# Strassen products for 14 of 22 column chunks of two FFN projections, with their weight sums made by DMA

## The chip, the cores and the metric

The kernel runs on one core of a Trainium2 chip. The metric is device time in microseconds for one launch; the time before is the median of three runs.

## The reference

Two transformer blocks run one after the other on one sequence of 512 tokens with 1024 features. The change lies in the gated feed-forward part, which occurs twice (layer 0 and layer 1):

```python
def conv_gated_ffn(x, w_up, w_gate, conv_w, conv_b, w_down):
    u = x @ w_up
    g = causal_dwconv(x @ w_gate, conv_w, conv_b)
    return (jax.nn.silu(g) * u) @ w_down
```

Here `x` is 512 x 1024, `w_up` and `w_gate` are 1024 x 2816, `w_down` is 2816 x 1024, and the convolution has three taps along the tokens. Everything is float32.

## The kernel before

**Layout.** Activations lie transposed: features on the 128 partitions, tokens along the row. `X` has 8 chunks of 128 features (index `k`), and 2816 columns are 22 chunks of 128 (index `f`). Every float32 operand is split into a rounded high part and a rest (`XH`, `XL`; `wh`, `wl`), and one product of a 128 x 128 weight block is three matmuls: high x high, high x low, low x high. `block` issues these three.

**The weight stream.** All weight blocks are laid out in HBM in the order in which TensorE (PE) uses them (`weight_order`, `ffn_order`), eight blocks (a unit, 512 KB) at a time. SyncE (SP) loads unit u into one of three buffers `wraw`, once unit u-3 has been split. ScalarE (ACT) rounds it to `wh` (`round_to`), VectorE (DVE) subtracts to get `wl` and raises the semaphore `w_lo`; there are four slots of `wh`/`wl`. Both engines do so at fixed places of their own programs: `feed_group` over blocks makes the unit three ahead (`AHEAD`) wherever the listed blocks cross the start of a unit. So a unit is split late if the engine is held up by the work written ahead of it.

**The FFN.** For each f PE makes 8 blocks of `up` and 8 blocks of `gate` into two of six PSUM banks. Then comes what I call the gating of f: ACT applies the middle tap to the gate bank, DVE adds the other two taps (two operations), ACT applies Silu, DVE multiplies by the up bank, ACT rounds the result to `HH`, DVE subtracts to get `HL`. The FFN is preceded by a projection `pg` (64 blocks), and by a layer norm, whose sums over the chunks are added by GpSimd (POOL) into `acc_s` as the chunks of `X` appear, then summed over the partitions by PE (`means`).

**Order.** All five programs are written out by hand, each engine runs its own strictly in order, and they meet at semaphores alone.

Of the kernel before, what the change touches and what calls it, by code (L numbers as in the profile page):

```python
# [15 lines left out]
KD = 8  # L16
# [5 lines left out]
ALPHA = 4.0 ** 0.25  # L22
TAPS = 31
# [100 lines left out]
class Stream:  # L124


    def __init__(self):
# [33 lines left out]
    def depth(self, m):  # L161
        return FT if m[:4] == "down" else 2 if m[:2] in ("pp", "uq") else 1 if m[:3] == "ukv" else KD
# [84 lines left out]
class Semaphores:  # L247
    def __init__(self, new):
# [13 lines left out]
        self.first_in, self.blank = n("first_in"), n("blank")  # L262
# [20 lines left out]
            n("f_u"), n("f_conv"), n("f_silu"), n("f_h"), n("f_hi"), n("f_lo"))  # L283

# [51 lines left out]
def place(nc, ctx, m):  # L336
# [47 lines left out]
    m.PP, m.HH, m.HL, m.pts = [], [], [], []  # L384
    for layer in range(2):
        with ExitStack() as ph:
            with ExitStack() as same:
                m.PP.append(sb(same, f"PP{layer}", [128, KD, S]))
            m.HH.append(sb(ph, f"HH{layer}", [128, FT, S], FR))
            with ExitStack() as same:  # L390
                m.pts.append(sb(same, f"pts{layer}", [128, 2, S]))
            m.HL.append(sb(ph, f"HL{layer}", [128, FT, S], FR))
# [26 lines left out]
    with ExitStack() as ph:  # L419
# [15 lines left out]
        m.pick, m.pick2 = sb(ph, "pick", [128, 128], FR), sb(ph, "pick2", [128, 128], FR)  # L435
    m.sba = [[sba[:, c] for _, c, _ in GR], [x[:, 0:c.stop - c.start] for x, (_, c, _) in zip((m.sqr[0], m.acc_q, m.acc_s), GR)]]
# [42 lines left out]

def unit(m, w, u):  # L480
# [7 lines left out]
def sync_program(sp, m, s, w, a):  # L488
    def raw(u):
# [4 lines left out]
        sp.e.dma_start(m.wraw[u % RAW][:, :], a["wstream"][u]).then_inc(s.raw[u % RAW], 16)  # L494
# [8 lines left out]
    def pt(layer):  # L503
        for k in range(2):
            sp.e.dma_start(m.pts[layer][:, k, :], a["pt"][layer][:, k * S:(k + 1) * S]).then_inc(s.pt_in[2 * layer + k], 16)

    x(0, 1, s.x_in[0])
    first(0, s.first_in)
# [7 lines left out]
    sp.e.dma_start(m.prm[:, :], a["params"]).then_inc(s.p_in, 16)  # L516
    sp.e.dma_start(m.cst[:, :], a["consts"]).then_inc(s.c_in, 16)
    for u in range(3, w.units):
# [12 lines left out]
        if u == w.at["in0", 0, 0] // NU + AHEAD + RAW:  # L531
            sp.wait_ge(s.nrm_u, normed(4, 7))
            for r in range(64, 128, 16):
                sp.e.dma_start(m.wgu[r:r + 16, :, :], a["wgu"].rearrange("l p n -> p l n")).then_inc(s.g_in, 16)
# [8 lines left out]
    for c in range(KD):  # L543
        sp.wait_ge(s.xsum, 48 + c + 1)
        sp.e.dma_start(a["o"][:, c * S:(c + 1) * S], m.X[:, c, :]).then_inc(s.out, 16)
    sp.wait_ge(s.out, 16 * KD)


def tensor_program(pe, m, s, w):
# [142 lines left out]
    def ffn(layer, i):  # L692
# [18 lines left out]
        for f in range(FT):  # L711
            bu, bg = bank[(2 + 2 * f) % 6], bank[(3 + 2 * f) % 6]
            if f < 3:
                pe.wait_ge(s.pg_u, 8 * layer + 4 + 2 * f)
# [4 lines left out]
            if f >= 3:  # L719
# [52 lines left out]
    pe.wait_ge(s.blank, 1)  # L772
# [539 lines left out]
def scalar_program(act, m, s, w, nc):  # L1312
# [92 lines left out]
    def embed_in(layer):  # L1405
        for k in range(2):
            act.wait_ge(s.pt_in[2 * layer + k], 16)
            fn(m.HH[layer][:, FT - 2 + k, :], m.pts[layer][:, k, :], ACT.Copy).then_inc(s.pt_hi, 1)

    def ffn(layer, i):  # L1410
# [9 lines left out]
        for f in range(FT):  # L1420
            n = FT * layer + f
            u, v = tmp[2 * f % 4], tmp[(2 * f + 1) % 4]
            bg = bank[(3 + 2 * f) % 6]
            feed_group(f"up{layer}", range(KD), [f])
            feed_group(f"gate{layer}", range(KD), [f])
            act.wait_ge(s.stream, w.done(f"gate{layer}", KD - 1, f))
# [1679 lines left out]
```

## Time and profile before

| | |
|---|---|
| median of three runs | 1748.67 us (1748.43 to 1748.83) |
| span of the profiled execution | 1747.5 us |
| what the median has over that span | 1.2 us |
| PE busy | 1736.9 us (99%) |
| DVE busy | 1063.6 us (61%) |
| ACT busy | 847.1 us (48%) |
| POOL busy | 18.4 us (1%) |
| granted TensorE clock | 1.000 |
| DMA, mean | 89 GB/s |

The span is from the first to the last instruction of one execution. Durations below come from that execution, and a difference of spans is set on the median. The busy time of PE is the union of overlapping matmuls, so the pace of PE is read from the distance between the starts of two matmuls, not from the duration of one.

### The profile page before, as it was taken

To read this page: it belongs to the slowest core of one execution; us is meant where nothing else is said; L and a number is where in the kernel's file an instruction comes from. 1 tells how busy PE (TensorE), PEld (TensorE's weight loads), DVE (VectorE), ACT (ScalarE), POOL (GpSimd) and SP (SyncE) were. 2 spreads that over 40 slices of the span, in tenths; PEclk is the share of its full clock that TensorE was granted. 3 is DMA by queue.
4 is the path that set the end of the run, shared out by engine and by line. 5 is a ranking of instruction groups with operands and counts; after the bars stand their busy time and mean duration, and the time that the engine had idled before them with its cause. 6 is when DMAs were issued, how large, how long until landed. Compare 5 with 4: busy or idle time off the path is not lost.

```text
span 1747.5 us, 22538 instructions
## 1 busy us (share of the span) xinstructions
PE 1736.9 (99%) x9213; PEld 1409.7 (81%) x9213; DVE 1063.6 (61%) x1666; ACT 847.1 (48%) x1330; POOL 18.4 (1%) x21
## 2 busy tenths in 40 slices
PE   9999999999999999999999999999999999999999
PEld 7887988888888897777778888888898866778766
DVE  6788864444433465877784444443378866656674
ACT  7789643333332355666463333342255455534542
POOL 0000100000000000000200000000000000000000
PEclk9999999999999999999999999999999999999999
DMA  5331232222222321111132232323213221132111
GB/s 216 110 121 45 89 109 97 97 97 97 97 97 96 97 85 61 62 58 51 61 112 96 96 98 95 101 90 109 97 61 107 96 70 63 61 97 97 61 60 49
DMA packets 44678, 155.43 MB, mean 89 GB/s; under 512 B 5280, under 2 KB 5536, under 8 KB 44576
## 3 DMA queue, kind: packets, MB, share of 16 engines
q1 hardware_dynamic: 44576, 153.99, 26.6%
q8 instruction: 73, 1.20, 0.3%
q14 instruction: 29, 0.24, 0.0%
HBM read 149.78 MB, written 2.10 MB: 87 GB/s over the span
## 4 chain that ended last, share of the span: by engine, by line
PE 90%; ACT 4%; DVE 4%; issue 1%; DMA 1%; SPq 0%; DVEq 0%; ACTq 0%
PE bank L553 89%; ACT tmp L1316 2%; DVE tmp L1990 1%; DVE wl L1999 1%; DMA wraw<-in_wstream 1%; ACT taps L1316 1%; ACT wh L1316 1%; PE bank L1261 0%; DVE XL L1999 0%; DVE sbl L1999 0%; ACT HL L1316 0%; DVE HL L1999 0%; ACT Y L1316 0%; DVE X L1987 0%; DVE acc_q L1987 0%
## 5 line engine op out<-in xcount | busy, mean ns | idle before, releaser
L553 PE MATMUL bank<-XH,wh 128*128 128x512 f32 (+1 forms) x1504 | 583.4, 388 | 3.7 <-ACT wh L1316 1.1
L553 PE MATMUL bank<-XL,wh 128*128 128x512 f32 (+1 forms) x1504 | 573.5, 382 | 0.0
L553 PE MATMUL bank<-XH,wl 128*128 128x512 f32 (+1 forms) x1504 | 573.5, 382 | 0.0
L1999 DVE TENSOR_TENSOR wl<-wraw,wh 128x1024 fp32r<-128x1024 f32 (+1 forms) x264 | 319.6, 1220 | 237.8 <-ACT wh L1316 237.2
L1316 ACT ACTIVATE wh<-wraw 128x1024 fp32r<-128x1024 f32 (+1 forms) x264 | 276.2, 1052 | 250.4 <-PE bank L553 242.7
L553 PEld LDWEIGHTS bank<-XH,wh 128*128 128x128 f32 x1504 | 282.8, 188 | 68.7 <-issue 9.3
L553 PEld LDWEIGHTS bank<-XH,wl 128*128 128x128 f32 x1504 | 282.8, 188 | 55.2
L553 PEld LDWEIGHTS bank<-XL,wh 128*128 128x128 f32 x1504 | 283.0, 188 | 52.3 <-issue 0.7
L1987 DVE SCALAR_TENSOR_TENSOR tmp<-bank,prm,tmp 128x511 f32<-128x511 f32 x88 | 65.9, 749 | 172.1 <-ACT tmp L1316 170.6
L553 PE MATMUL bank<-HH,wh 128*128 128x512 f32 (+1 forms) x420 | 155.7, 371 | 0.0
L553 PE MATMUL bank<-HH,wl 128*128 128x512 f32 (+1 forms) x420 | 154.1, 367 | 0.0
L553 PE MATMUL bank<-HL,wh 128*128 128x512 f32 (+1 forms) x420 | 154.0, 367 | 0.0
L1316 ACT ACTIVATE tmp<-bank,prm 128x512 f32<-128x512 f32 (+1 forms) x64 | 46.2, 723 | 193.0 <-PE bank L553 192.9
L1316 ACT ACTIVATE tmp<-tmp 128x512 f32<-128x512 f32 (+2 forms) x131 | 72.4, 595 | 86.3 <-DVE tmp L1987 85.8
L553 PEld LDWEIGHTS bank<-HH,wh 128*128 128x128 f32 x420 | 79.2, 189 | 13.8 <-issue 0.6
L553 PEld LDWEIGHTS bank<-HL,wh 128*128 128x128 f32 x420 | 79.2, 189 | 13.5 <-issue 0.5
L553 PEld LDWEIGHTS bank<-HH,wl 128*128 128x128 f32 x420 | 79.2, 189 | 13.0
L1316 ACT ACTIVATE tmp<-bank 128x512 f32<-128x512 f32 (+4 forms) x129 | 70.8, 567 | 17.8 <-PE bank L553 15.3
L1990 DVE TENSOR_TENSOR X<-X,bank 128x512 f32<-128x512 f32 (+1 forms) x58 | 38.5, 665 | 40.0 <-PE bank L553 40.0
L553 PE MATMUL bank<-XH,HL 128*128 128x256 f32 x256 | 57.4, 287 | 0.3 <-DVE XL L1999 0.2
L553 PE MATMUL bank<-wh,XH 128*128 128x512 f32 x128 | 50.7, 396 | 0.1
L553 PE MATMUL bank<-wh,XL 128*128 128x512 f32 x128 | 49.9, 390 | 0.0
(350 smaller groups left out, 2181.9 us busy)
## 6 DMA issues: line engine op xcount, KB each, us to landing
wraw<-in_wstream SPq DMA_DIRECT2D x276, 512.0 KB, 3.5
out<-X SPq DMA_DIRECT2D x8, 256.0 KB, 2.3
X<-in_xt SPq DMA_DIRECT2D x3, 512.0 KB, 8.9
pts<-in_pt SPq DMA_DIRECT2D x4, 256.0 KB, 3.7
eb<-lab SPq DMA_DIRECT2D x16, 64.0 KB, 2.0
cst<-in_consts SPq DMA_DIRECT2D x1, 810.5 KB, 10.1
X<-in_xt SPq DMA_DIRECT2D x2, 256.0 KB, 4.2
wraw<-in_wstream SPq DMA_DIRECT2D x2, 256.0 KB, 4.8
```

Source lines behind the costliest of these rows:

```text
L553: return pe.e.matmul(o, l, r, start=start, stop=stop, skip_group_check=True)
L1316: return act.e.activation(o, i, f, **kw)
L1987: return dve.e.scalar_tensor_tensor(out=o, in0=i0, scalar=sc, in1=i1, op0=op0, op1=op1)
L1990: return dve.e.tensor_tensor(o, i0, i1, op)
L1999: return dve.e.tensor_tensor(o, x, h.bitcast(F32), ALU.subtract)
```

## The change

For the first 14 chunks (seven pairs f, f+1) of both projections, the 2 x 2 product of halves is made with seven quarter products instead of eight. The halves are: features 0 to 511 and 512 to 1023, tokens 0 to 255 and 256 to 511, chunk f and chunk f+1. A quarter product is four blocks on 256 tokens. Three things are needed for it:

- **Sums of weights.** Four arrays T1 to T4 are formed in HBM (`tw`) by POOL's DMA queue. For each layer there are eleven transfers of one quarter of the weights of all 14 pairs of both matrices (14 x 128 x 512 floats, 3.67 MB): four copies, then four, two and one that accumulate, each stage waiting for the one before. They stand in POOL's program ahead of the sums of the layer norm. The stream then takes the blocks `tu` and `tg` from `tw`, and SP waits for all eleven ahead of the first of them.
- **Sums of activations.** DVE forms four sums of quarters of X (`SF`, `SG`), ACT and DVE split them into `XS`, in rows of `HH` and `HL` that the FFN does not use yet.
- **Combining.** Per pair and matrix, ACT copies two quarters out of PSUM, DVE does five additions of 256 tokens, and the results lie in SBUF (`sqr` for up, `acc_s` and `acc_q` for gate). The gating reads them there in place of the banks, and is done for both chunks of a pair in the next pair.

The blocks of a pair go from 32 on 512 tokens to 56 on 256 tokens, so the units of the stream go from 4 to 7 a pair.

```diff
 def ffn_order(layer):
     out = []
-    for f in range(FT):
+    for p in range(PAIRS):
+        f, (up, gate), (tu, tg) = 2 * p, (f"up{layer}", f"gate{layer}"), (f"tu{layer}", f"tg{layer}")
+        out += [(up, k, f) for k in range(KD)]
+        if p:
+            out += [(gate, k, f - 1) for k in range(4, KD)]
+        out += [(tu, k, p) for k in range(16)] + [(gate, k, f) for k in range(KD)]
+        out += [(up, k, f + 1) for k in range(4, KD)] + [(tg, k, p) for k in range(16)]
...
 def sync_program(sp, m, s, w, a):
...
-        sp.e.dma_start(m.wraw[u % RAW][:, :], a["wstream"][u]).then_inc(s.raw[u % RAW], 16)
+        for c0, c1, summed in w.pieces(u):
+            if summed:
+                mat, k, p = w.order[NU * u + c0 // 128]
+                layer = int(mat[2:])
+                sp.wait_ge(s.tw, 176 * (layer + 1))
+                src = a["tw"][k // 4, layer, p + PAIRS * (mat[1] == "g")]
...
 def tensor_program(pe, m, s, w):
...
+        def last_product(g, p):
+            pe.wait_ge(s.u_c, combined(layer, p, g, 3))
+            pe.wait_ge(s.xs_l, 4 * layer + 4)
+            product(("up", "gate")[g] + str(layer), 2 * p + 1, 4, bank[3 * g + 1][:, lo], sums_of(3), False, True)
+
+        for p in range(PAIRS):
+            first_products(0, p)
+            if p:
+                last_product(1, p - 1)
+            summed_products(0, p)
+            first_products(1, p)
+            last_product(0, p)
+            summed_products(1, p)
...
 def vector_program
...
+        for p in range(PAIRS):
+            f = 2 * p
+            feed_group(up, range(KD), [f])
+            if p:
+                gated(f - 2, sqr[0], m.gb[0])
+            first_combined(0, p)
+            if p:
+                feed_group(gate, range(4, KD), [f - 1])
+                last_combined(1, p - 1)
+                gated(f - 1, sqr[1], m.gb[1])
+            feed_group(tu, range(16), [p])
+            three_combined(0, p)
+            feed_group(gate, range(KD), [f])
+            first_combined(1, p)
+            feed_group(up, range(4, KD), [f + 1])
+            last_combined(0, p)
+            dve.wait_ge(s.u_c, combined(layer, p, 0, 5))
+            feed_group(tg, range(16), [p])
+            three_combined(1, p)
...
 def gpsimd_program
+    def weight_sums(layer):
+
+        t1, t3, t4, t2 = (a["tw"][t, layer].rearrange("n p c -> (n p) c") for t in range(4))
+        w11, w12, w21, w22 = (a[n][layer].rearrange("n p c -> (n p) c") for n in ("w11", "w12", "w21", "w22"))
+        pool.wait_ge(s.w_lo, (6, 60)[layer])
+        for t in (t1, t3, t2, t4):
+            pool.e.dma_start(t, w12).then_inc(s.tw, 16)
+        pool.wait_ge(s.tw, 176 * layer + 64)
+        for t, x in ((t1, w11), (t3, w22), (t2, w22), (t4, w22)):
+            pool.e.dma_start(t, x, accum_op=ALU.add, max_dma_last_dim=8192).then_inc(s.tw, 16)
+        pool.wait_ge(s.tw, 176 * layer + 128)
+        for t in (t2, t4):
+            pool.e.dma_start(t, w11, accum_op=ALU.add, max_dma_last_dim=8192).then_inc(s.tw, 16)
+        pool.wait_ge(s.tw, 176 * layer + 160)
+        pool.e.dma_start(t4, w21, accum_op=ALU.add, max_dma_last_dim=8192).then_inc(s.tw, 16)
```

The programs of DVE in the FFN of layer 0 show what now lies in a row. Before, in the stretch of two chunks (one pair), four splits of units (`wl`) and two gatings:

```order
L1999 TENSOR_TENSOR wl1<-wraw1,wh1 128x1024 [waits s_w_hi]
L1999 TENSOR_TENSOR wl2<-wraw2,wh2 128x1024 [waits s_w_hi]
L1987 SCALAR_TENSOR_TENSOR tmp0<-bank1,prm,tmp0 128x511 [waits s_f_u]
L1987 SCALAR_TENSOR_TENSOR tmp0<-bank1,prm,tmp0 128x510 [waits s_dve]
L1990 TENSOR_TENSOR tmp1<-tmp0,bank0 128x512 [waits s_f_silu]
L1999 TENSOR_TENSOR HL0<-tmp1,HH0 128x512 [waits s_f_hi]
```

After, the same engine from the last addition behind one pair's `tg` blocks to the point at which the next pair's `up` blocks of chunk f+1 may start (the first two rows of `three_combined(0, p)` stand last):

```order
L2140 TENSOR_TENSOR acc_s<-acc_s,bank5 128x256
L2149 TENSOR_TENSOR wl3<-wraw2,wh3 128x1024 [waits s_w_hi]
L2137 SCALAR_TENSOR_TENSOR tmp0<-acc_s,prm,tmp0 128x511 [waits s_f_u]
L2137 SCALAR_TENSOR_TENSOR tmp0<-acc_s,prm,tmp0 128x510 [waits s_dve]
L2140 TENSOR_TENSOR tmp1<-tmp0,sqr0 128x512 [waits s_f_silu]
L2149 TENSOR_TENSOR HL0<-tmp1,HH0 128x512 [waits s_f_hi]
L2140 TENSOR_TENSOR sqr0<-sqr0,bank0 128x256 [waits s_u_e]
L2140 TENSOR_TENSOR acc_q<-bank4,acc_q 128x256 [waits s_stream]
L2137 SCALAR_TENSOR_TENSOR tmp2<-acc_q,prm,tmp2 128x511 [waits s_f_u]
L2137 SCALAR_TENSOR_TENSOR tmp2<-acc_q,prm,tmp2 128x510 [waits s_dve]
L2140 TENSOR_TENSOR tmp3<-tmp2,sqr1 128x512 [waits s_f_silu]
L2149 TENSOR_TENSOR HL0<-tmp3,HH0 128x512 [waits s_f_hi]
L2149 TENSOR_TENSOR wl0<-wraw0,wh0 128x1024 [waits s_w_hi]
L2149 TENSOR_TENSOR wl1<-wraw1,wh1 128x1024 [waits s_w_hi]
L2140 TENSOR_TENSOR sqr0<-sqr1,bank1 128x256 [waits s_u_e]
L2140 TENSOR_TENSOR sqr1<-bank1,sqr0 128x256 [waits s_u_c]
```

Both gatings now stand in one row of DVE's program, with three splits and four additions, ahead of the two additions on which PE waits.

POOL's program, from its start, which had nothing ahead of the first `acc_s` row before:

```order
L3152 DMA tw<-in_w12 64x14336 [waits s_w_lo]
L3152 DMA tw<-in_w12 64x14336 x3
L3155 DMA tw<-in_w11 448x2048 [waits s_tw]
L3155 DMA tw<-in_w22 448x2048 x3
L3158 DMA tw<-in_w11 448x2048 [waits s_tw]
L3158 DMA tw<-in_w11 448x2048
L3160 DMA tw<-in_w21 448x2048 [waits s_tw]
L3136 ISA
L3136 TENSOR_TENSOR acc_s<-X 128x512 [waits s_nrm_u,s_xsum]
```

The layer norm's first sum now stands behind the wait for ten of the eleven transfers.

## Rows read from the trace of the kernel before

**Rows 1.** The page: the span, and busy time of each engine

```profile
span 1747.5 us, 22538 instructions
PE 1736.9 (99%) x9213; PEld 1409.7 (81%) x9213; DVE 1063.6 (61%) x1666; ACT 847.1 (48%) x1330; POOL 18.4 (1%) x21
```

**Rows 2.** The page's chain that ended last, by engine and by line

```profile
PE 90%; ACT 4%; DVE 4%; issue 1%; DMA 1%; SPq 0%; DVEq 0%; ACTq 0%
PE bank L553 89%; ACT tmp L1316 2%; DVE tmp L1990 1%; DVE wl L1999 1%; DMA wraw<-in_wstream 1%; ACT taps L1316 1%; ACT wh L1316 1%; PE bank L1261 0%; DVE XL L1999 0%; DVE sbl L1999 0%; ACT HL L1316 0%; DVE HL L1999 0%; ACT Y L1316 0%; DVE X L1987 0%; DVE acc_q L1987 0%
```

**Rows 3.** Timeline of PE in the FFN (start us, duration us): matmuls of 512

```profile
336.78 0.39 PE L553 MATMUL bank<-XH,wl 128*128 128x512 f32 x1
337.01 0.39 PE L553 MATMUL bank<-XH,wh 128*128 128x512 f32 x1
```

**Rows 4.** Timeline of PE near 163 us: matmuls of 256, 24 apart

```profile
162.80 0.28 PE L553 MATMUL bank<-XH,HL 128*128 128x256 f32 x1
...
165.68 0.28 PE L553 MATMUL bank<-XH,wl 128*128 128x256 f32 x1
```

**Rows 5.** Timeline of DVE in the FFN, one chunk and the next gating

```profile
338.02 1.54 DVE L1987 SCALAR_TENSOR_TENSOR tmp<-bank,prm,tmp 128x511 f32<-128x511 f32 x2 [3.88 <-ACT tmp L1316]
...
341.64 0.69 DVE L1999 TENSOR_TENSOR HL<-tmp,HH 128x512 fp32r<-128x512 f32 x1 [0.70 <-ACT HH L1316]
342.59 2.43 DVE L1999 TENSOR_TENSOR wl<-wraw,wh 128x1024 fp32r<-128x1024 f32 x2 [0.26 <-ACT wh L1316]
348.90 1.53 DVE L1987 SCALAR_TENSOR_TENSOR tmp<-bank,prm,tmp 128x511 f32<-128x511 f32 x2 [3.88 <-ACT tmp L1316]
351.13 0.69 DVE L1990 TENSOR_TENSOR tmp<-tmp,bank 128x512 f32<-128x512 f32 x1 [0.70 <-ACT tmp L1316]
352.52 0.69 DVE L1999 TENSOR_TENSOR HL<-tmp,HH 128x512 fp32r<-128x512 f32 x1 [0.70 <-ACT HH L1316]
```

**Rows 6.** Timeline of ACT, the first step of the same gatings

```profile
337.21 0.78 ACT L1316 ACTIVATE tmp<-bank,prm 128x512 f32<-128x512 f32 x1 [4.32 <-PE bank L553]
348.09 0.78 ACT L1316 ACTIVATE tmp<-bank,prm 128x512 f32<-128x512 f32 x1 [4.32 <-PE bank L553]
```

**Rows 7.** Groups by shape over the span, DVE and ACT (busy us, mean ns)

```profile
L1999 DVE TENSOR_TENSOR wl<-wraw,wh 128x1024 fp32r<-128x1024 f32 x262 | 318.2, 1224 | 237.3 <-ACT wh L1316 236.6
L1987 DVE SCALAR_TENSOR_TENSOR Y<-cin,prm,Y 128x512 f32<-128x512 f32 x16 | 12.0, 752 | 0.3
L1990 DVE TENSOR_TENSOR X<-X,bank 128x256 f32<-128x256 f32 x4 | 1.7, 418 | 8.3 <-PE bank L553 8.3
L1316 ACT ACTIVATE acc_s<-bank 128x256 f32<-128x256 f32 x8 | 3.0, 379 | 0.0
```

**Rows 8.** The page on DMA: the queue of the stream, issue to landing

```profile
q1 hardware_dynamic: 44576, 153.99, 26.6%
wraw<-in_wstream SPq DMA_DIRECT2D x276, 512.0 KB, 3.5
```

**Rows 9.** Windows: busy of each engine, clock, DMA share, GB/s

```profile
30.00:178.00 148.00, 146.33 (x1151) 117.80 (x1144) 119.86 (x174) 125.37 (x195) 0.00 (x0) 1.00 0.28 92
250.00:440.00 190.00, 190.00 (x840) 157.39 (x839) 94.07 (x109) 71.40 (x89) 0.00 (x0) 1.00 0.29 95
```

**Rows 10.** Timeline of POOL in the layer norm ahead of layer 0's FFN

```profile
178.36 1.30 POOL L2926 TENSOR_TENSOR acc_s<-X 128x512 f32<-128x512 f32 x1 [177.92 <-DVE X L1987]
181.42 1.68 POOL L2926 TENSOR_TENSOR acc_s<-acc_s,X 128x512 f32<-128x512 f32 x1 [1.76 <-DVE X L1987]
186.37 1.73 POOL L2926 TENSOR_TENSOR acc_s<-acc_s,X 128x256 f32<-128x256 f32 x2 [0.96 <-DVE X L1987]
```

**Rows 11.** Timeline of PE: the sum of `acc_s` over the partitions

```profile
190.97 0.59 PE L553 MATMUL bank<-acc_s,cst 128*128 128x256 f32 x2
```

**Rows 12.** Timeline of DVE: splits of units 6 and 7, and ahead of layer 0's FFN

```profile
29.18 2.35 DVE L1999 TENSOR_TENSOR wl<-wraw,wh 128x1024 fp32r<-128x1024 f32 x2
...
226.15 2.35 DVE L1999 TENSOR_TENSOR wl<-wraw,wh 128x1024 fp32r<-128x1024 f32 x2
...
234.00 2.35 DVE L1999 TENSOR_TENSOR wl<-wraw,wh 128x1024 fp32r<-128x1024 f32 x2
```

**Rows 13.** Timeline of ACT: it waits for PE to leave a slot

```profile
244.79 1.06 ACT L1316 ACTIVATE wh<-wraw 128x1024 fp32r<-128x1024 f32 x1 [4.38 <-PE bank L553]
```

More of the change, by code:

```diff
@@ L22 @@
 ALPHA = 4.0 ** 0.25
+PAIRS = 7
+XS0 = 14
 TAPS = 31
@@ L42, in ffn_order @@
     out = []
-    for f in range(FT):
+    for p in range(PAIRS):
[5 more added lines that the diff above has]
+        out += [(up, k, f + 1) for k in range(4, KD)] + [(tg, k, p) for k in range(16)]
+    f = 2 * PAIRS
+    out += [(f"up{layer}", k, f) for k in range(KD)] + [(f"gate{layer}", k, f - 1) for k in range(4, KD)]
+    out += [(f"gate{layer}", k, f) for k in range(KD)]
+    for f in range(2 * PAIRS + 1, FT):
         out += [(f"up{layer}", k, f) for k in range(KD)] + [(f"gate{layer}", k, f) for k in range(KD)]
@@ L170, in done, with pieces, landed @@
         return self.total[p] - (3 - i if self.incs[p] == 4 else 0)
+    def pieces(self, u):
+        sums = [(b := self.order[NU * u + 4 * h]) is not None and b[0][:2] in ("tu", "tg") for h in range(2)]
+        return [(0, NU * 128, False)] if not any(sums) else [(512 * h, 512 * h + 512, sums[h]) for h in range(2)]
+    def landed(self, u):
+        return 16 * sum(len(self.pieces(v)) for v in range(u % RAW, u + 1, RAW))
     def used(self, u):
@@ L221, in half_at, with sums_of_pair, combined @@
     return sum(TAIL[j] + SPLIT[j] for j in range(1, i) if PARTS[j] == 2 and j != 3)
+def sums_of_pair(p):
+    return [(p, 0, 1)] + [(p - 1, 1, 5)] * (p > 0) + [(p, 0, 2), (p, 0, 3), (p, 0, 4), (p, 1, 1), (p, 0, 5), (p, 1, 2), (p, 1, 3), (p, 1, 4)]
+SUMS = [x for p in range(PAIRS) for x in sums_of_pair(p)] + [(PAIRS - 1, 1, 5)]
+def combined(layer, p, mat, j):
+    return 10 * PAIRS * layer + SUMS.index((p, mat, j)) + 1
 def normed(i, f):
@@ L388, in place @@
                 m.PP.append(sb(same, f"PP{layer}", [128, KD, S]))
+                m.SF.append([x[:, i, :, :] for x in [sb(same, f"SF{layer}", [128, 3, 4, 256])] for i in range(3)])
             m.HH.append(sb(ph, f"HH{layer}", [128, FT, S], FR))
@@ L391, in place @@
                 m.pts.append(sb(same, f"pts{layer}", [128, 2, S]))
+                sb(same, f"between{layer}", [128, 6, S])
+                m.SF[layer].append(sb(same, f"SG{layer}", [128, 4, 256])[:, :, :])
             m.HL.append(sb(ph, f"HL{layer}", [128, FT, S], FR))
@@ L435, in place @@
         m.pick, m.pick2 = sb(ph, "pick", [128, 128], FR), sb(ph, "pick2", [128, 128], FR)
+    m.XS = [[(m.HH, m.HL)[j // 2][layer][:, XS0 + 4 * (j % 2):XS0 + 4 * (j % 2) + 4, :] for j in range(4)] for layer in range(2)]
+    m.gb = [m.acc_s, m.acc_q]
     m.sba = [[sba[:, c] for _, c, _ in GR], [x[:, 0:c.stop - c.start] for x, (_, c, _) in zip((m.sqr[0], m.acc_q, m.acc_s), GR)]]
@@ L710, in ffn, with product @@
                     block(f"pg{layer}", k, c, bank[c][:, :], XH[:, k, :], XL[:, k, :], k == 0, k == KD - 1)
[L711 to L714, printed above, removed]
-            else:
+        lo, hi = slice(0, 256), slice(256, 512)
+        def product(mat, c, k0, o, x, first, last):
+            for k in range(k0, k0 + 4):
+                xh, xl = x(k)
+                block(mat, k, c, o, xh, xl, first and k == k0, last and k == k0 + 3)
@@ L716, in ffn @@
+        for f in range(2 * PAIRS, FT):
+            bu, bg = bank[(2 + 2 * f) % 6], bank[gate_bank(f)]
+            if f == 2 * PAIRS:
+                pe.wait_ge(s.u_c, combined(layer, PAIRS - 1, 0, 5))
+            elif f == 2 * PAIRS + 1:
+                pe.wait_ge(s.u_e, 4 * PAIRS * (layer + 1))
+                pe.wait_ge(s.u_c, 10 * PAIRS * (layer + 1))
+            elif f >= 2 * PAIRS + 3:
                 pe.wait_ge(s.f_h, FT * layer + f - 2)
@@ L1419, in ffn, with gated @@
                 fn(tmp[c % 4][:, :], bank[c][:, :], ACT.Sigmoid).then_inc(s.pg_u, 1)
-        for f in range(FT):
+            if f0 == 0:
+                for j in range(4):
+                    act.wait_ge(s.xs_f, 4 * layer + j + 1)
+                    fn(m.XS[layer][j][:, :, 0:256], m.SF[layer][j], ACT.Copy).then_inc(s.xs_h, 1)
+        up, gate, tu, tg = f"up{layer}", f"gate{layer}", f"tu{layer}", f"tg{layer}"
+        def gated(f, g):
             n = FT * layer + f
             u, v = tmp[2 * f % 4], tmp[(2 * f + 1) % 4]
[L1423 to L1426, printed above, removed]
             act.wait_ge(s.pg_x, 8 * layer + 8)
@@ L3014, in lay_out @@
     for n, w in enumerate(order):
-        if w is not None:
+        if w is not None and w[0][:2] not in ("tu", "tg"):
             m, k, c = w
```

168 lines of the change are left out of this document (137 added, 31 removed).

## The prediction

> **What bounds the kernel now.** I read the page first: PE is busy for 1736.9 of 1747.5 us, while DVE has 61% and ACT 48% [rows 1]. The chain that ended last says the same, 90% of it is PE, 89% one line, the matmul helper [rows 2]. So time is gained only by giving PE less to do, and lost as soon as another engine makes PE wait. Next I read the pace of PE from the starts of its matmuls. In the FFN, DVE's first tap of one chunk starts at 338.02 and that of the next at 348.90, so a chunk takes 10.88 us for its 48 matmuls of 512 tokens, 0.2267 us each; two neighbouring starts, 336.78 and 337.01, agree [rows 3, 5]. Matmuls of 256 tokens run 24 in 2.88 us, 0.120 us each [rows 4]. In the FFN PE is busy without a gap, 190.00 of 190 us; DVE is busy for half of it [rows 9].
>
> **What PE saves.** Per pair and matrix there were 16 blocks x 3 x 0.2267 = 10.88 us, now 28 x 3 x 0.120 = 10.08 us. The 256-token matmul costs 53% of the 512 one, so of the eighth that Strassen saves not quite 7.4% is left. Both matrices: 21.76 down to 20.16 us a pair, 14 pairs in two layers, 22.4 us if nothing ever waits.
>
> **DVE's row in a pair.** From the order of the programs: PE may start the last product of `up` (4 blocks) only when DVE has done the first two additions of `three_combined(0, p)`, and these stand behind both gatings of the pair before. The row starts when PE ends the 16 blocks of `tg`. Let that be 0, and price each step:
> - ACT copies a quarter out of PSUM: 0.20 us until it starts (the matmul that starts at 336.78 gives its place up at 337.01, ACT starts at 337.21 [rows 3, 6]), 0.38 for the copy [rows 7], 0.05 to reach DVE: 0.63.
> - Three additions of 256, at 0.42 [rows 7], 1.3 with their own waits.
> - One split of a unit. It occupies DVE for 1.22, and the next can start after 1.15: 1.15. ACT's rounding is done under the additions, and so is its first tap.
> - The gating of the first chunk, from DVE's first tap at 348.90 to the end of its last step at 353.21: 4.31, of it two waits of 0.70 for ACT [rows 5]. The taps read SBUF now; a tap from SBUF takes 0.752, from a bank 0.77, so that gives nothing [rows 5, 7].
> - Two additions of 256: 0.8.
> - The gating of the second chunk. ACT's first tap needs the addition just made, so it counts from ACT's start, 348.09 to 353.21: 5.12, and 0.08 for the handover [rows 5, 6].
> - Two splits: in the rows the two end 2.70 us after the gating before them (342.33 to 345.02), since ACT rounds them only after its part of the gating [rows 5].
> - Two additions: 0.9. Then 0.1 to PE.
>
> The sum is 0.63 + 1.3 + 1.15 + 4.31 + 0.8 + 5.2 + 2.7 + 0.9 + 0.1 = 17.1 us. PE reaches the same point after 8 blocks of `up`, 4 of `gate`, 16 of `tu` and 8 of `gate`, 36 x 0.36 = 12.96 us. It waits 4.1 us. After that it has 4 + 16 blocks to the end of `tg`, 7.2 us, and the row starts again; DVE's work in that part (four splits, three additions, 6.2 us) is hidden under it. So a pair takes 24.3 us, a closed loop of DVE and PE, against 21.76 before. What had covered the gating before was that nothing on DVE was needed by PE before the banks came round, a whole chunk later (DVE waited 3.88 us per chunk [rows 5]).
>
> Per layer: the first pair has no gating ahead of it and runs at PE's pace, 52 x 0.36 = 18.7 us. Six pairs take 6 x 24.3 = 145.8. The last product of `gate` is 1.4. Together 165.9 against 7 x 21.76 = 152.3, **+13.6 us a layer, +27 in both**. The eight chunks left run as before.
>
> **Sums of activations.** Four additions and four subtractions of 1024 elements on DVE, 8 x 1.22 = 9.8 us, stand ahead of the split that starts at 234.00 [rows 7, 12]. That unit is then ready at 234.0 + 9.8 + 1.2 = 245.0. PE ends its units at ACT's waits, 244.79 less some 0.1, and needs it there [rows 13]: 0.3 us. I take 1 us for both layers; it would be 10 us a layer if that cover were gone.
>
> **Sums of weights.** They start when the sixth unit has been split. The two splits at 29.18 are the sixth and seventh, so at 30.4 us [rows 12]. POOL can begin the layer norm's sums when ten transfers have landed, 36.7 MB. It began them at 178.36, and PE used the sum at 190.97; POOL's last addition had ended at 188.10, so 2.9 us are spare [rows 10, 11]. No row shows a transfer from HBM to HBM, nor one that accumulates. Bounds:
> - From below: a byte costs what it costs the stream. 153.99 MB took 26.6% of 1747.5 us, 331 GB/s at full use [rows 1, 8]. 36.7 MB are 111 us, and the stream takes 0.28 of the engines meanwhile [rows 9], so 154 us: done at 184 us. POOL's row of 1.3, 1.7, 1.7 and 0.9 follows: 190. PE waits for nothing.
> - From above: an accumulating transfer fetches what lies there too, so its bytes count twice. 14.7 + 2 x 22.0 = 58.7 MB are 177 us. From 30.4 to 191 us, 0.72 x 161 = 116 of them get done; then PE stands, the stream stops, and 61 are left: 252 us, POOL's row to 258, PE late by 67 us.
>
> I take the upper one, rounded to 60, because the sum cannot be made without reading both. A delay here is not made up: PE is always busy. The eleventh transfer is done some 22 us after the tenth and the stream asks for it later: before, the unit three behind it was split at 228.5 [rows 12], 37 us after PE's place at 190.97, so it costs nothing more.
>
> The Trainium skill, page "DMA: Bandwidth & Descriptors", section "Latency and other measured facts", has copies between two HBM tensors at 207 to 214 GB/s at best. An estimate from it: 36.7 MB, each byte once, would be 172 us, 116 of them by 191, the rest to 247 us, a delay of 62 us even if accumulation cost nothing. No run so far shows that rate; it speaks for the upper bound, by another way.
>
> **Layer 1's sums** start at the sixtieth unit, in the third pair of layer 0's FFN. In a pair of 24.3 us the stream now moves 7 units (3.67 MB), 151 GB/s or 0.46 of 331, where it took 0.29 before [rows 9]; a unit lands 3.5 us after its issue [rows 8]. DVE splits the last units of a pair in a burst with some 4 us for a load, so a landing twice as long costs 1 to 2 us a pair: 5 us in all, between 0 and the crowding below. They end long before layer 1's layer norm, some 540 us later.
>
> **Sum.** 27 + 1 + 60 + 5 = 93 on the span of 1747.5, which with its 1.2 is the median: **about 1842 us**.
>
> **The rivals.**
> - *The transfers are in time, DVE's loop alone costs:* 1748.7 + 28 = 1777 us. It needs the lower bound of the rate. Chance 0.22.
> - *The transfers crowd the stream.* A copy is cut into 64 rows of 57 KB, an accumulating one into rows of 8 KB (the order shows 64x14336 and 448x2048), the stream's packets are 153.99 MB / 44576 = 3.5 KB [rows 8]. If an engine takes one piece of each in turn, the stream has 4/61 of the engines while the copies run (14.7 MB, 44 us): two units land where layer 1's copies meet a demand of 13. With 3 in hand that is 8 x 3.5 = 27 us; in layer 0, at 5.44 us a unit, some 16. Beside the accumulating ones the stream gets 1/3, 110 GB/s, or 1/5, 66 GB/s, against 151: on some 22 units 1.3 to 4.5 us each, 29 to 98 us. Together 1842 + 72 to 140, 1914 to 1982 us. For it: nothing but the sizes. Against it: if the engines share by bytes, the stream's half (165 GB/s) is enough. Chance 0.15. (The Trainium skill, same page, section "Queues, rings and completion order": an engine goes round its queues packet by packet. That is this rival's rule; no row here has two busy queues.)
> - *Faster.* PE never waits in a pair: 1748.7 - 22 = 1726 us. It needs the row of 17.1 us to shrink to 12.96, and all transfers in time; the change breaks even at a row of 14.6 us. Nothing in the rows is 2.5 us shorter than I took it, the seven long waits and operations are read straight from the same code. Chance 0.09.
> - *No change,* by a row of 14 to 15 us and transfers in time: 0.04.
>
> **How the numbers follow.** The forecast, a delay of 40 to 80 us beside DVE's loop, has 0.50: 1815 to 1865. A range for 8 in 10 takes in the first rival, half the way to the second's upper end: 1765 to 1935. A measurement of this kernel tells about 0.2% from no change (3.5 us): faster 0.09, the same 0.04, slower 0.87.
>
> **What would show it.** In the profile after: PE's idle time before the first matmul of `up`'s last product (`HL` as the moving operand, 256 tokens) in each pair, released by DVE's additions, some 4 us each, twelve times; gatings of one pair back to back on DVE; starts of `tg` rows 24.3 us apart. POOL's first `acc_s` row at 240 to 255 us instead of 178, and PE standing for about 60 us at the sum of `acc_s`. Landings of the stream longer than 3.5 us between 30 and 250 us. I am wrong if POOL's first row stays near 180 (then 1777), or if gaps show before matmuls whose releaser is a split of a unit or a DMA (then crowding, above 1900).

## The result, and the profile after

The changed kernel takes 1977.41 us (median of four runs, 1975.26 to 1978.57), against 1748.74 for the one before on the same chip. The ratio is 1.1306, 95% interval 1.129 to 1.1322: 13% slower, 229 us. I had said 1842, with 1935 as the upper end.

The page after, the lines that answer to [rows 1, 2, 8]:

```profile
span 1975.3 us, 25036 instructions
...
PE 1771.6 (90%) x10221; PEld 1490.1 (75%) x10221; DVE 1179.4 (60%) x1864; ACT 914.7 (46%) x1436; POOL 36.5 (2%) x43
...
PEclk9898999866789999999999998899999999999999
...
q1 hardware_dynamic: 60704, 176.02, 27.6%
q0 software_dynamic: 7136, 80.74, 16.9%
...
PE 69%; DMA 15%; DVE 9%; ACT 5%; issue 1%; SPq 0%; POOL 0%; ACTq 0%; DVEq 0%; POOLq 0%
```

PE is busy for 90% of the span instead of 99%, and 15% of the chain that ended last is now DMA, which had 1% in [rows 2]. A new queue, q0, stands beside the stream's q1: POOL's transfers. The row of the granted clock, which read 9 throughout before, falls to 6 in the ninth and tenth of the 40 slices, and that is where PE stands most.

To see where the 229 us went, I set the same work side by side at two places that every kernel here has: POOL's first addition of each layer norm. POOL's timeline after (start, duration, the wait ahead in brackets):

```profile
31.72 2.19 POOL L3152 DMA_DIRECT2D tw<-in_w  x4 [31.27 <-DVE wl L2149]
80.81 4.03 POOL L3155 DMA_DIRECT2D tw<-in_w  x4 [46.91 <-DMA tw<-in_w]
172.41 1.97 POOL L3158 DMA_DIRECT2D tw<-in_w  x2 [87.56 <-DMA tw<-in_w]
214.67 0.97 POOL L3160 DMA_DIRECT2D tw<-in_w  x1 [40.29 <-DMA tw<-in_w]
225.91 1.29 POOL L3136 TENSOR_TENSOR acc_s<-X 128x512 f32<-128x512 f32 x1 [10.27 <-DVE X L2137]
...
364.36 2.04 POOL L3152 DMA_DIRECT2D tw<-in_w  x4 [108.44 <-DVE wl L2149]
413.63 4.01 POOL L3155 DMA_DIRECT2D tw<-in_w  x4 [47.23 <-DMA tw<-in_w]
...
1060.50 1.30 POOL L3136 TENSOR_TENSOR acc_s<-X 128x512 f32<-128x512 f32 x1 [519.85 <-DVE X L2140]
```

The first sum starts at 225.91 instead of 178.36 [rows 10]: 47.5 us are lost before layer 0's FFN. But look at what released it. It waited 10.27 us for DVE's `X`; ten transfers had landed at 214.67, eleven us earlier. So POOL's place in the order, my term of 60 us, did not bind. Between the two sums lie 834.6 us; before, 684.4. The rest of the kernel, with layer 1's FFN in it, lost another 30 us.

The same kernel's DMA window from 31 to 81 us, while the four copies run:

```profile
q0 software_dynamic: 320, 14.68, 81.2%
q1 hardware_dynamic: 606, 2.23, 14.9%
...
wraw<-in_wstream SPq DMA_DIRECT2D x6, 512.0 KB, 24.1
```

And the chain that ended last, its first DMA steps (start, duration):

```profile
32.56 25.39 DMA wraw<-in_wstream
60.32 22.84 DMA wraw<-in_wstream
85.53 17.98 DMA wraw<-in_wstream
...
365.59 47.57 DMA wraw<-tw
415.97 16.95 DMA wraw<-tw
435.28 29.15 DMA wraw<-in_wstream
```

Six units of the stream were loaded in 50 us with a median of 24.1 us from the issue of a load to its landing (the moment at which all of it has arrived), where [rows 8] have 3.5; the kernel before loaded ten in the same window. PE waits at a landing again and again. That is the crowding, my rival with 0.15. In layer 0's pairs one load from `tw`, half a unit (256 KB), took 47.57 us. PE's share there, by windows:

```profile
365.00:562.00 197.00, 80.39 (x504) 78.26 (x504) 53.31 (x77) 36.25 (x50) 8.37 (x10) 0.66 1.01 261
1123.00:1298.00 175.00, 149.09 (x1123) 146.92 (x1121) 116.54 (x165) 83.24 (x115) 0.00 (x0) 0.91 0.44 138
1189.70:1194.50 4.80, 4.77 (x22) 4.77 (x23) 3.33 (x5) 1.06 (x1) 0.00 (x0) 0.50 0.87 295
1194.50:1201.50 7.00, 7.00 (x60) 7.00 (x60) 3.54 (x5) 3.17 (x4) 0.00 (x0) 1.00 0.49 160
```

The columns are window, length, PE, PEld, DVE, ACT, POOL, granted clock, DMA share, GB/s. While layer 1's transfers run, PE works 80 of 197 us, at a mean clock of 0.66, and the DMA engines are full at 261 GB/s. The second window is some six pairs of layer 1, where no transfer of POOL's runs. There the pair as such can be seen, in PE's timeline:

```profile
1189.73 0.80 PE L606 MATMUL bank<-HL,wh 128*128 128x256 f32 x2 [4.35 <-DVE sqr L2140]
...
1216.70 0.80 PE L606 MATMUL bank<-HL,wh 128*128 128x256 f32 x2 [4.37 <-DVE sqr L2140]
```

The wait stands where I put it, released by whom I said, 4.35 us long where I had 4.1. But a pair takes 26.97 us, not 24.3. The last two windows show the missing part: in the 4.8 us behind the wait the granted clock is 0.50, the lower of its two levels (1.2 GHz), and PE gets 22 matmuls done; in the next 7 us it is 1.00, with 60 matmuls.

### The profile page after: what moved, and what is told of

Same layout as the page of the kernel before. It is cut to its first block, busy times and chain, and to the rows that moved or that the text cites. A ratio compares the mean times of both kernels' runs of the same rounds, so it can differ in the third digit from the quotient of the medians.

```text
span 1975.3 us, 25036 instructions
## 1 busy us (share of the span) xinstructions
PE 1771.6 (90%) x10221; PEld 1490.1 (75%) x10221; DVE 1179.4 (60%) x1864; ACT 914.7 (46%) x1436; POOL 36.5 (2%) x43
## 4 chain that ended last, share of the span: by engine, by line
PE 69%; DMA 15%; DVE 9%; ACT 5%; issue 1%; SPq 0%; POOL 0%; ACTq 0%; DVEq 0%; POOLq 0%
PE bank L606 68%; DMA wraw<-in_wstream 10%; DMA wraw<-tw 5%; DVE wl L2149 3%; ACT wh L1425 2%; ACT tmp L1425 2%; DVE tmp L2137 1%; DVE tmp L2140 1%; DVE sqr L2140 1%; DVE HL L2149 0%; PE bank L1370 0%; ACT HH L1425 0%; DVE acc_q L2140 0%; ACT taps L1425 0%; DVE X L2137 0%
## 5 line engine op out<-in xcount | busy, mean ns | idle before, releaser
L606 PE MATMUL bank<-XH,wh 128*128 128x512 f32 (+1 forms) x1392 | 507.7, 365 | 8.9 <-DVE wl L2149 6.4
L606 PE MATMUL bank<-XL,wh 128*128 128x512 f32 (+1 forms) x1392 | 497.3, 358 | 0.0
L606 PE MATMUL bank<-XH,wl 128*128 128x512 f32 (+1 forms) x1392 | 496.8, 357 | 0.0
L606 PE MATMUL bank<-HL,wh 128*128 128x256 f32 (+1 forms) x868 | 255.6, 345 | 145.3 <-DVE acc_q L2140 79.3
L606 PEld LDWEIGHTS bank<-HL,wh 128*128 128x128 f32 x868 | 163.6, 210 | 162.0 <-DVE acc_q L2140 80.0
L606 PE MATMUL bank<-HH,wh 128*128 128x256 f32 (+1 forms) x868 | 254.4, 344 | 6.6 <-DVE sqr L2140 3.3
L606 PE MATMUL bank<-HH,wl 128*128 128x512 f32 (+1 forms) x644 | 224.3, 348 | 0.0
L606 PEld LDWEIGHTS bank<-HH,wh 128*128 128x128 f32 x868 | 162.3, 209 | 21.2 <-DVE sqr L2140 3.5
L1425 ACT ACTIVATE tmp<-bank 128x512 f32<-128x512 f32 (+4 forms) x129 | 70.4, 566 | 15.4 <-PE bank L606 13.2
L606 PE MATMUL bank<-HL,wl 128*128 128x256 f32 x224 | 71.5, 319 | 0.0
L606 PEld LDWEIGHTS bank<-HL,wl 128*128 128x128 f32 x224 | 51.4, 229 | 0.0
```

Source lines behind the costliest of these rows:

```text
L606: return pe.e.matmul(o, l, r, start=start, stop=stop, skip_group_check=True)
L1425: return act.e.activation(o, i, f, **kw)
```

## The experiments

Where a number of a kernel is compared with its neighbour's, both are read at the same places: "front" is the start of the first `acc_s` sum in layer 0, "middle" the distance from it to that of layer 1, which holds layer 0's FFN. Before they are 178.36 and 684.4, after 225.91 and 834.6. "Kernel 1" is the kernel of experiment 1, and so on. Kernels 2, 3, 7, 9 and 10 were run once each, so their small differences carry little: the change and kernel 7 have the same program up to the 60th unit, and still their fronts are 8 us apart.

**1. Without the transfers.** `tu` and `tg` are read straight from quarters of the weights in HBM, not summed, so that the products of the pairs are of other numbers; everything on the engines stays.

```diff
-                sp.wait_ge(s.tw, 176 * (layer + 1))
-                src = a["tw"][k // 4, layer, p + PAIRS * (mat[1] == "g")]
+                src = a[("w11", "w12", "w21", "w22")[k // 4]][layer, p + PAIRS * (mat[1] == "g")]
...
-        weight_sums(i // 2)
```

> The changed kernel without the eleven transfers that sum the weights: the tu and tg blocks are read from the unsummed quarters in HBM, so their products are of other weights. What is left is DVE's row in each pair and what TensorE's clock does after a wait. Theory A, the row and the clock: layer 0 costs what layer 1 costs in the changed kernel's trace, 30 us each, pairs of 27 us, 1809 us. Theory B, the row alone as I forecast: pairs of 24.3 us, 1777 us. Rival C, that the transfers only hid a gain: 1726 us.

1809.18 us (1808.73 to 1809.89), 1.0344 of before, interval 1.0326 to 1.0361. Front 178.16, middle 714.5. So the transfers cost 168 us (48 in the front, 120 in the middle), and the pairs alone make the kernel 60 us slower. Some 6 of the 120 us fall ahead of layer 1's transfers, beside the last of layer 0's: the change splits its 60th unit 138 us behind its front (POOL's row at 364.36), kernel 1 the same unit 132 us behind its own. Beside layer 1's transfers it is 114.

**2. The transfers alone,** in the kernel before, their result unused.

```diff
+    def weight_sums(layer):
...
     for i in (1, 3):
+        weight_sums(i // 2)
```

> The kernel before with the eleven transfers a layer on POOL's queue at the same places, their result unused. Theory A, the transfers crowd the stream whoever uses it: +52 us ahead of layer 0's FFN as in the changed kernel, and about as much again in layer 0's FFN, whose units are used 5.44 us apart as in the convolution: 1853 us. Rival, that the stream of seven units a pair is what could not be fed: +52 us ahead of the FFN, under 20 us in it, under 1820 us. Rival, POOL's late sum of the layer norm: its first row would wait for the transfers and not for DVE.

1831.71 us, one run. Front 226.48, 48 us late like the change. Middle 718.4, 34 more than before, where I had expected about 52. So the front's loss is whole without any Strassen product, but the middle's is not: beside plain chunks the middle loses 34 us, beside pairs 120. Of the 34, 5 lie ahead of the second set: it starts 161 us behind the front, and in kernels 8 and 9 below, which have no transfers in the front, 156 us behind it.

**3. Copies in smaller rows,** 8 KB in place of 57 KB.

```diff
-            pool.e.dma_start(t, w12).then_inc(s.tw, 16)
+            pool.e.dma_start(t, w12, max_dma_last_dim=8192).then_inc(s.tw, 16)
```

> The changed kernel with the four copies of a layer cut into rows of 8 KB instead of 57 KB. Theory A, an engine takes a piece of each queue in turn: the stream's share in the copies' 49 us goes from 10 to 15% up to a third, a unit lands in 8 to 11 us instead of 24, and some 20 us are won in the convolution and 25 to 30 in the FFN: 1925 to 1935 us. Rival, the engines share by bytes or by queue, whatever the pieces: 1977 us, landings of 24 us.

1947.97 us, one run, 29 us less than the change, where I had expected 42 to 52 less. The DMA window from 31 to 81 us:

```profile
q0 software_dynamic: 1686, 13.42, 73.5%
q1 hardware_dynamic: 1152, 4.19, 24.3%
...
wraw<-in_wstream SPq DMA_DIRECT2D x9, 512.0 KB, 10.5
```

The same engines with the same demand, and the stream now moves 4.19 MB instead of 2.23, landing in 10.5 us instead of 24.1. Nothing but the size of a row on the other queue differs. The accumulating transfers, which had rows of 8 KB already, still crowd. In the change, while the four of them run (81 to 172 us):

```profile
q0 software_dynamic: 1856, 14.68, 78.5%
...
wraw<-in_wstream SPq DMA_DIRECT2D x14, 512.0 KB, 15.4
```

Of the 29 us won only 8 lie in the front. There POOL's first sum now starts at once behind the issue of the eleventh transfer and waits for no `X`:

```profile
217.46 0.97 POOL L3160 DMA_DIRECT2D tw<-in_w  x1 [41.24 <-DMA tw<-in_w]
218.17 1.67 POOL L3136 TENSOR_TENSOR acc_s<-X 128x512 f32<-128x512 f32 x1
```

So POOL's place in the order begins to bind, though the chain that ended last still goes through the stream's landings here (one of 12.46 us from 201.87).

**4. The low clock, filled in.** Kernel 1, in which PE makes 34 idle matmuls of 256 into a free bank ahead of the wait for DVE.

```diff
+            if g == 0 and p:
+                for _ in range(34):
+                    mm(bank[7][:, lo], m.identb[:, :], m.identb[:, 0:1].broadcast_to([128, 256]), True, True)
             pe.wait_ge(s.u_c, combined(layer, p, g, 3))
```

> The kernel without the transfers (e1), and PE fills its wait ahead of the last product of up, in each pair but the first, with 34 idle matmuls of 256 tokens (4.1 us) into a bank that nobody reads. Theory A, the wait drops TensorE's clock and this costs 2.3 us a pair: pairs of 24.5 to 24.7 us, 1809 - 28 = 1781 us, granted clock 1.00. Rival, the clock does not matter or the fill only delays: the same 1809 us or more.

1783.47 us (1782.96 to 1784.47), a clock of 1.000. PE does more work and the kernel is 25.7 us faster than kernel 1. PE's waits for DVE's `sqr`, of kernel 1 and of this one:

```profile
PE bank L605 <- DVE sqr L2139: 52.6, 13, 4.4
```

```profile
PE bank L605 <- DVE sqr L2142: 7.1, 13, 0.6
```

So 25.7 us in 12 pairs, 2.1 us each, is what the clock costs behind a wait of 4.35 us; the wait itself stays, filled with idle work.

**5. DVE's row cut.** Kernel 1, the second gating of a pair written behind `three_combined(0, p)` and `first_combined(1, p)`, on ACT and DVE, with a second buffer for up's result in turns; nothing is computed differently.

```diff
             if p:
                 feed_group(gate, range(4, KD), [f - 1])
                 last_combined(1, p - 1)
-                gated(f - 1, sqr[1], m.gb[1])
             feed_group(tu, range(16), [p])
             three_combined(0, p)
             feed_group(gate, range(KD), [f])
             first_combined(1, p)
+            if p:
+                gated(f - 1, (sqr[1], m.alt[layer])[(p - 1) % 2], m.gb[1])
```

> The kernel without transfers, with the second gating of a pair written behind the three additions of up and the first addition of gate, on ACT and DVE alike; nothing is computed differently. If the wait of 4.35 us is DVE's row of two gatings, it shrinks to some 2 us: what stands ahead of PE's point is one gating, three splits and four additions, and the second gating delays the next point instead. A pair is then 22.6 us where it was 26.9 (wait and low clock together): 1809 - 12 x 4.3 = about 1757 us. If the wait is set by something that does not move with the gating (the bank being read out, the order of splits), it stays at 1809.

1749.83 us (median of ten runs, nine of them from 1749.10 to 1751.76; one took 5999.56, for which I have no cause), a ratio of 1.0006 to before, interval 0.9996 to 1.0016: 59 us less than kernel 1, somewhat more than the 52 forecast. PE's waits for `sqr` are 2.0 us at most and the clock is 0.999:

```profile
PE bank L606 <- DVE sqr L2141: 11.3, 11, 2.0
```

One gating's place in the programs of ACT and DVE was worth nearly all that the pairs cost, the clock included.

**6. The waits inside a gating filled.** The same, and splits of units and additions written between a gating's steps, where DVE and ACT wait for each other.

```diff
         def gated(f, bu, bg, a=lambda: None, b=lambda: None):
...
             stt(u[:, 2:S], bg[:, 0:S - 2], P(f"fcw{layer}", 3 * f), u[:, 2:S], ALU.mult, ALU.add).then_inc(s.f_conv, 1)
+            a()
             dve.wait_ge(s.f_silu, n + 1)
             tt(v[:, :], u[:, :], bu[:, :], ALU.mult).then_inc(s.f_h, 1)
+            b()
             dve.wait_ge(s.f_hi, n + 1)
```

> The kernel before this one, and splits of units and additions written into the places at which DVE and ACT wait for each other inside a gating. DVE's work in a pair is then about 17.5 us without its own waits, less than PE's 20.16, so PE should wait for almost nothing and keep its clock: a pair of 20.2 to 20.8 us, 1809 - 12 x 6.3 = about 1733 us, 1726 at best. This is the figure that the products alone can give, if the sums of weights cost nothing. If PE cannot make use of 256-token matmuls at 0.12 us over a whole pair (a limit of its own, not DVE's), it stays above 1748.

1735.68 us (1735.31 to 1737.12), 0.9927 of before, interval 0.9913 to 0.9942. This is what the products can give if the sums of weights cost nothing: 13 us, of the 22.4 that PE's pace allows. The waits for `sqr`:

```profile
PE bank L606 <- DVE sqr L2145: 6.6, 13, 0.5
```

**7. Layer 1's transfers behind the pairs.** The changed kernel, with the second set started at the 112th unit.

```diff
-        pool.wait_ge(s.w_lo, (6, 60)[layer])
+        pool.wait_ge(s.w_lo, (6, 112)[layer])
```

> The changed kernel with the transfers of layer 1 started at the 112th unit in place of the 60th, behind the last pair of layer 0. Theory: the crowding costs most where the stream's demand is high (7 units in a pair of some 24 us, each late at the same place where PE has no slack), about 114 us in the pairs, and about 30 us beside plain chunks (the kernel before with the transfers alone showed that). Then 1977 - 114 + 30 = about 1893 us. Rival: the cost is that of the transfers wherever they lie (bytes taken from the stream), then it stays within 1960 to 1985.

1913.32 us, one run, where I had expected 1893. Its span is 64 us shorter than the change's. The front was 8 us later than the change's (233.82) with the same program up to there, which I did not trace; the middle is 760.8, 46 us over kernel 1 where the change is 120 over it. Here too some 3 of the 46 lie ahead of the second set. So the same bytes in the same rows cost 46 us beside plain chunks and `down`, 120 beside pairs. The rival, a fixed price for the bytes, is out; my 30 was too little, 43 would have been right.

**8 and 9. Pairs in layer 1 alone,** in the order of kernel 6, with real sums; layer 0's FFN as before. Its eleven transfers start at the 60th unit beside plain chunks, in rows of 2 KB (8), or of 57 and 8 KB as in the change (9).

```diff
+PN = (0, 7)
...
-    for p in range(PAIRS):
+    for p in range(PN[layer]):
...
-            pool.e.dma_start(t, w12).then_inc(s.tw, 16)
+            pool.e.dma_start(t, w12, max_dma_last_dim=2048).then_inc(s.tw, 16)
```

> Seven-product pairs in layer 1 alone, in the order that left PE almost without waits; layer 0 as in the kernel before. Layer 1's eleven transfers run in rows of 2 KB, from the 60th unit on, beside plain chunks, with some 480 us until they are needed. The order gives 13.2 us for fourteen pairs, 6.6 for seven: about 1742 us if the stream is not crowded, faster than before by 0.4%. It holds if the engines take one piece of each queue in turn, since the stream's pieces (3.5 KB) are then the larger ones and its demand is 0.29 of them. Rival: the bytes crowd the stream whatever their pieces; the kernel before with the transfers lost about 30 us in this place, so about 1772 us. If POOL's own time for many small pieces counts, the layer norm's sums are late and it is above both.

> The same kernel with the transfers cut as in the change (copies in rows of 57 KB, accumulating ones in rows of 8 KB). If pieces taken in turn are the cause of the crowding, it loses what the kernel before lost with its transfers in this place, about 30 us over the one with 2 KB rows: about 1772 us, the stream's landings some 25 us beside the copies. If the bytes are the cause, it is as fast as the one with 2 KB rows, within 5 us.

With 2 KB rows: 1741.79 us (1741.47 to 1742.94, five runs), 0.9962 of before, interval 0.9948 to 0.9975. It is the fastest of the kernels here that sum the weights, and 0.4% faster than before. With wide rows: 1769.49, one run. The windows over the transfers, first of 8, then of 9:

```profile
334.00:600.00 266.00, 266.00 (x1203) 221.56 (x1202) 114.24 (x127) 85.53 (x101) 15.11 (x11) 1.00 0.96 250
```

```profile
334.00:560.00 226.00, 204.31 (x878) 164.32 (x877) 87.86 (x99) 69.55 (x85) 8.82 (x11) 0.98 0.98 267
```

In both the DMA engines are as good as full (0.96 and 0.98) and move some 250 GB/s. In one PE never stands, in the other it stands 22 us and the mean clock is 0.98. "The engines are busy" is thus not the cause; how long a unit takes to land is. The landings in the window 365 to 415, first of 8, then of 9:

```profile
wraw<-in_wstream SPq DMA_DIRECT2D x9, 512.0 KB, 9.0
```

```profile
wraw<-in_wstream SPq DMA_DIRECT2D x7, 512.0 KB, 17.5
```

The stream runs three units ahead. In plain chunks a unit lasts PE 5.44 us, so a landing may take some 16 us (3 x 5.44) before PE waits: 9.0 is inside it, 17.5 is not.

**10. The changed kernel with rows of 2 KB.**

> The changed kernel with all its transfers in rows of 2 KB, nothing else changed. If the engines take one piece of each queue in turn, the stream gets half of them or more when it asks, its landings stay under 8 us and the crowding is gone: what is left is DVE's row and the low clock (1809 us, as without the transfers) and POOL's first sum behind transfers that now take longer, done at 220 to 250 us, so 30 to 60 us at the layer norm: 1840 to 1870 us. If the bytes are the cause it stays above 1940, as with copies in rows of 8 KB.

1901.56 us, one run, 76 less than the change, and some 30 more than expected. Its front is 240.94, its middle 742.9: 62.8 and 28.4 over kernel 1. Against the change the front is 15 us later and the middle 92 us shorter, so what small rows win here they win in layer 0's pairs. POOL's timeline and the chain that ended last at the front:

```profile
239.88 1.67 POOL L3160 DMA_DIRECT2D tw<-in_w  x1 [20.21 <-DMA tw<-in_w]
240.94 1.98 POOL L3136 TENSOR_TENSOR acc_s<-X 128x512 f32<-128x512 f32 x1
```

```profile
147.83 48.07 DMA tw<-in_w
...
218.00 21.48 DMA tw<-in_w
241.62 1.32 POOL acc_s L3136
```

Here the mechanism that I had forecast for the change is the one that binds: with the stream no longer held up, the chain goes through POOL's transfers `tw` and its sum, which starts at 240.94 without a wait for DVE, 62.8 us late. Two things expected failed: landings were to stay under 8 us and took 12.4 in the window 31 to 81, and the middle should have been free and costs 28. In a pair PE takes a unit in 20.16 / 7 = 2.9 us, so three units ahead are less than 9 us, and the chain's steps of loads in the pairs, once the transfers have started, are mostly 7 to 14 us long:

```profile
376.80 14.42 DMA wraw<-in_wstream
...
405.15 10.05 DMA wraw<-in_wstream
417.57 12.24 DMA wraw<-in_wstream
```

What costs nothing beside plain chunks (kernel 8) costs beside pairs.

## Why the prediction was wrong

**The step that failed** is in the weight sums: the stream "takes 0.28 of the engines meanwhile", so that the transfers get 0.72 and PE runs on undisturbed until POOL's late sum. I let the stream have what it asked for, and gave the new queue the rest. It went the other way. Beside copies in 57 KB rows the stream got 0.149 of the engines, and PE, which had no idle time to give, waited for the stream. The tenth transfer had then landed sooner than I had it (214.67 instead of 252), and the late sum was hidden behind a PE that was late already: the front is 48 us late, but by landings. The same assumption priced layer 1's transfers: "a landing twice as long", 7 us, and 5 us in all. Those landings took 17.8 and 20.0 us, and the middle lost 120. Besides, my bound from above made PE 67 us late, and I had no ground to round that down to 60. Kernel 2 shows that this is the transfers' doing alone, kernels 3, 9 against 8, and 10 (29, 28 and 76 us) that the size of a row is a large part of it.

**The sum, term by term.**

| term | predicted, us | measured, us | from |
|---|---|---|---|
| DVE's loop and PE's pace, both layers | +27 | +35 | kernel 4 against before |
| sums of activations | +1 | 0 | windows of kernel 1 |
| low clock behind the wait | 0 | +26 | kernel 1 against 4 |
| ahead of layer 0's FFN | +60 | +48 | front, change against kernel 1 |
| layer 1's transfers | +5 | +120 (6 ahead of their start) | middle, change against kernel 1 |
| all | +93 | +229 | |

- *Layer 1's transfers* is the term that was mis-sized most. I had the demand of a pair right and took a landing twice as long; between 414 and 560 us the loads of `tu` and `tg` landed in 20.0 us and those of whole units in 17.8, where I had 7:

```profile
wraw<-tw SPq DMA_DIRECT2D x20, 256.0 KB, 20.0
```

The rival's 29 to 98 us for the accumulating ones, with 27 for the copies, covers the 120 at its upper end (8 units at 3.5 us are 28, not 27; it changes nothing). Its total, 1914 to 1982, held the result, though it kept my 60 for a late sum beside 16 of crowding in the front; the measured front was 48 in all. I had set its chance low with "for it: nothing but the sizes". The sizes were the evidence.
- *That an accumulating transfer counts twice* holds roughly. The four copies took 31.72 to 80.81, 14.68 MB at 299 GB/s; the four accumulating ones of the same size 80.81 to 172.41, 160 GB/s. But their rows are 57 and 8 KB. In kernel 3, where all are 8 KB, the two stages took 57.4 and 86.0 us, a factor of 1.5. By the use of the engines (81.2% of 50 us against 78.5% of 91) it is 1.76, and the ten transfers come to an estimated 148 us of full use, where my bound from above had 177: the other reason why they were done before 252. The rate that the Trainium skill gives in the page "DMA: Bandwidth & Descriptors", section "Latency and other measured facts", for copies between HBM tensors (207 to 214 GB/s at best, for tiles of 128 x 16 KiB) does not bound the copies here, which ran at 299, so the delay that I had worked out from it has no ground.
- *The rule on queues* from the same page, section "Queues, rings and completion order", that an engine goes round its queues packet by packet, has the right sign: with wide rows on the other queue the stream's landings go from 4.2 (before, same window) to 24.1 us. Read as "one row of each in turn" it goes too far. Rows of 57 KB against 3.5 would leave the stream 0.06 and it got 0.149; 8 KB and 2 KB rows gave landings of 10.5 and 12.4 us in the window 31 to 81, no better for the smaller ones. It is the rows of 57 KB that stand out there. What the 2 KB rows gained came later, beside the accumulating transfers, where 8 KB rows gave 15.4 us (81 to 172, above). Kernel 10 from 100 to 190 us:

```profile
wraw<-in_wstream SPq DMA_DIRECT2D x13, 512.0 KB, 7.7
```

- *DVE's row* was right in place, releaser and size. DVE's timeline in layer 1 has, from the first addition behind `tg` to the second one on which PE waits:

```profile
1173.22 0.41 DVE L2140 TENSOR_TENSOR acc_s<-acc_q,bank 128x256 f32<-128x256 f32 x1
...
1176.10 1.53 DVE L2137 SCALAR_TENSOR_TENSOR tmp<-acc_s,prm,tmp 128x511 f32<-128x511 f32 x2
...
1181.96 1.54 DVE L2137 SCALAR_TENSOR_TENSOR tmp<-acc_q,prm,tmp 128x511 f32<-128x511 f32 x2 [0.89 <-ACT tmp L1425]
...
1186.53 2.36 DVE L2149 TENSOR_TENSOR wl<-wraw,wh 128x1024 fp32r<-128x1024 f32 x2 [0.25 <-ACT wh L1425]
...
1189.26 0.42 DVE L2140 TENSOR_TENSOR sqr<-bank,sqr 128x256 f32<-128x256 f32 x1
```

That is 16.46 us; with the 0.63 of ACT's copy ahead of it that is the 17.1 us that I had summed. Kernels 5 and 6 take the row apart and the wait goes with it.
- *PE's pace* was right: in kernels 6 and 8 pairs run with waits of 0.5 us at most and the kernel is faster than before.
- *The missing term* is the clock. I priced a wait at its length. Here a wait of 4.35 us is followed by 4.8 us at half pace, 2.1 us more per pair, half as much again as the wait. The Trainium skill, page "TensorE: Matmul & The Clock Gate", section "HAM oscillation — how this bites in real kernels", describes this for matmul bursts between waits for DMA; the trace agrees, with its granted clock of 0.50 behind the wait shown, and waits of up to 2.0 us (kernel 5) left the clock at 0.999. I had looked at the clock of before only, which was 1.000 because PE never stood.
- *Sums of activations* cost nothing that the trace shows. DVE makes layer 0's at 228 us, and between 225 and 258 us PE is busy for 33.00 of 33 us in kernel 1 as in the kernel before, while DVE is busy for 29.8 us where it had 20.3; in layer 1, between 930 and 975 us of both, it is 45.00 of 45. Most of what the first row of the table has over the forecast is the pair itself: 26.97 less 2.14 for the clock is 24.83, 0.5 over my 24.3, 6 us in twelve pairs. Half of that 0.5 is the wait (4.35 for 4.1); the rest I did not trace.

**What the change would have needed.** The pairs can be had (kernel 6), the sums of layer 1 can be hidden beside plain chunks in small rows (kernel 8), those of layer 0 were not hidden in any rows tried: with accumulated bytes at 1.76 times they weigh as some 53 MB of copies beside a stream that PE lives on, and cost 40 to 63 us in the front (40 in kernel 3, 48 in the change, 63 in kernel 10), more than the 22 us that all pairs could bring. Another place for POOL's sum in kernel 10 was not tried. Where the sums are hidden, in layer 1 alone, the whole gain is 7 us.

## What to carry to other kernels

Before a second DMA queue is put beside a stream that feeds a busy engine, compare its landing time with what the stream has in hand (units ahead x time per unit), not the bandwidths: here a landing of 9 us where 16 were in hand cost nothing, and one of 17.5 cost 28 us, at the same use of the engines. Cut the background transfers into small rows, and put them where the stream's demand is lowest. And price a wait of TensorE with the clock that it loses: take from the trace what the matmuls behind a wait of that length cost; work moved from one row of an engine's program to another was worth more (59 us, 26 of them the clock) than the arithmetic that the change saved (22 at best).

## What the runs showed of the hardware that I had not expected

- A DMA queue with rows of 57 KB beside one with 3.5 KB packets raises the latter's landing from 4.2 to 24.1 us, at 0.81 and 0.15 of the engines; with 8 KB rows it is 10.5 us.
- Rows of 2 KB cost throughput in accumulating transfers: one of 3.67 MB took 28 to 30 us in kernel 8 (issues at 497.11, 526.84 and 554.64), two together 47 us in kernel 9 (475.40 to 522.71), and from the first issue to the last one it took 221 us, where the wide rows of kernel 9 took 189.
- Copies from HBM to HBM on POOL's queue ran at 299 GB/s beside the stream in rows of 57 KB and at 256 in rows of 8 KB (kernel 3), accumulating ones in rows of 8 KB at 160 and 171.
- A wait of TensorE of 4.35 us in 27 was enough for a clock of 0.50 in the following 4.8 us; idle matmuls in the wait avoided it and made the kernel 26 us faster.
